# Two transformer blocks on one core: weight parts ahead of waits, tiles taken out of PSUM by ScalarE, and sums of squares on TensorE

## What is computed

```
h = x                                     # 1024 tokens, 1024 channels, fp32
h = h + hybrid_mixer(rmsnorm(h)) ; h = h + cross_attention(rmsnorm(h), mem)
h = h + (gelu(causal_dwconv(u[..., :F])) * u[..., F:]) @ w_down ; u = rmsnorm(h) @ w_up
x2 = rmsnorm(h, final_g)                  # F = 2816 here and below
z = rms_norm(x2) @ w_in_2                 # sliding window attention and an HGRN2 recurrence
h = x2 + rms_norm(concat([ya, yh]) @ w_out_2, g_mix_post_2)
h = h + rms_norm(cross_attention_2(rms_norm(h), m), g_x_post_2)
u = rms_norm(h, g_ffn_pre_2)
h = h + rms_norm((silu(u @ w_gate_2) * (u @ w_up_2)) @ w_down_2, g_ffn_post_2)
```

## Time and profile before

| | us |
|---|---|
| median of 3 runs | 2897.3 |
| lowest and highest | 2895.75, 2897.48 |
| the profiled execution | 2897.78 |
| its span | 2895.9 |
| TensorE busy | 2764.6 |
| DVE busy | 1813.2 |
| GpSimd busy | 1378.6 |
| ScalarE busy | 1012.2 |
| mean granted TensorE clock | 0.977 of full |

### The profile page before, as it was taken

The page is one execution under the profiler, slowest core; times in us unless marked ns, Lnnn a source line. Parts: engine busy times, 40 slices in busy tenths (PEclk is TensorE's granted clock), DMA queues, the critical chain, the costliest instruction groups (busy, mean ns, idle before and its releaser), DMA issues.

```text
span 2895.9 us, 36440 instructions
## 1 busy us (share of the span) xinstructions
PE 2764.6 (95%) x13206; PEld 2282.4 (79%) x13206; DVE 1813.2 (63%) x1944; ACT 1012.2 (35%) x1605; POOL 1378.6 (48%) x789
## 2 busy tenths in 40 slices
PE   7999899999999999999999998899997999999996
PEld 6888687887788888888887776678976888888884
DVE  7888542335876676766745547694479555655556
ACT  3257531332322222223323435353446222222223
POOL 4322212214666676665565330434153666566665
PEclk9999999999999999999999998899998999999998
DMA  4101222111111111113322110422023111111113
GB/s 147 37 23 52 80 96 79 36 59 51 44 51 47 54 47 62 51 46 114 110 89 87 37 44 1 153 87 89 15 95 110 55 51 58 54 43 58 47 61 124
DMA packets 71982, 191.25 MB, mean 66 GB/s; under 512 B 7760, under 2 KB 8016, under 8 KB 70864
## 3 DMA queue, kind: packets, MB, share of 16 engines
q1 hardware_dynamic: 59616, 152.92, 15.9%
q10 hardware_dynamic: 12272, 37.06, 3.4%
HBM read 172.65 MB, written 17.30 MB: 66 GB/s over the span
## 4 chain that ended last, share of the span: by engine, by line
PE 48%; issue 34%; POOL 14%; DVE 2%; ACT 1%; DMA 1%; POOLq 0%; SPq 0%; DVEq 0%; ACTq 0%
PE products L649 15%; PE products L1078 8%; PE others L1078 8%; PE products L1120 5%; PE others L1120 5%; POOL w_lo L550 4%; POOL w_lo L494 2%; POOL w_hi L491 2%; POOL w_raw L568 1%; POOL w_raw L566 1%; DMA w_raw<-wstream 1%; DVE work L2233 1%; POOL w_raw L557 1%; POOL part_sum L562 1%; PE products L769 1%
## 5 line engine op out<-in xcount | busy, mean ns | idle before, releaser
L550 POOL TENSOR_TENSOR w_lo<-w_raw,w_hi 128x512 fp32r<-128x512 f32 x328 | 457.3, 1399 | 457.0 <-ACT w_hi L1780 455.9
L1780 ACT ACTIVATE w_hi<-w_raw 128x512 fp32r<-128x512 f32 x328 | 207.7, 634 | 816.5 <-PE others L1078 207.6
L491 POOL TENSOR_TENSOR w_hi<-w_raw,small 128x1024 fp32r<-128x1024 f32 x56 | 113.9, 2034 | 641.6 <-PE products L649 357.2
L649 PE MATMUL products<-act_hi,w_hi 128*128 128x512 f32 x912 | 366.7, 402 | 5.7 <-issue 4.4
L649 PE MATMUL products<-act_lo,w_hi 128*128 128x512 f32 x912 | 357.3, 392 | 0.0
L649 PE MATMUL products<-act_hi,w_lo 128*128 128x512 f32 x912 | 357.2, 392 | 0.0
L494 POOL TENSOR_TENSOR w_lo<-w_raw,w_hi 128x1024 fp32r<-128x1024 f32 x96 | 253.5, 2641 | 165.3 <-ACT w_hi L2065 160.9
L649 PEld LDWEIGHTS products<-act_hi,w_hi 128*128 128x128 f32 x912 | 172.4, 189 | 48.8 <-issue 12.5
L649 PEld LDWEIGHTS products<-act_hi,w_lo 128*128 128x128 f32 x912 | 172.4, 189 | 37.2
L649 PEld LDWEIGHTS products<-act_lo,w_hi 128*128 128x128 f32 x912 | 172.8, 189 | 33.3 <-issue 0.2
L743 PE MATMUL products<-act_hi,w_hi 128*128 128x512 f32 x408 | 170.6, 418 | 18.5 <-DVE act_lo L3114 8.1
(11 more groups left out here) (534 smaller groups left out, 6907.7 us busy)
## 6 DMA issues: line engine op xcount, KB each, us to landing
w_raw<-wstream SPq DMA_DIRECT2D x155, 512.0 KB, 3.5
w_raw<-wstream SPq DMA_DIRECT2D x248, 256.0 KB, 2.6
work<-xT ACTq DMA_DIRECT2D x16, 512.0 KB, 8.1
parked<-work ACTq DMA_DIRECT2D x8, 512.0 KB, 3.0
work<-parked ACTq DMA_DIRECT2D x8, 512.0 KB, 8.8
parked<-work ACTq DMA_DIRECT2D x2, 2048.0 KB, 7.9
work<-parked SPq DMA_DIRECT2D x8, 512.0 KB, 7.7
out<-work ACTq DMA_DIRECT2D x16, 256.0 KB, 2.2
```

The costliest lines, as they stand in the source:

```text
L491: pool.tensor_tensor(w_hi[:, slot, :], w_raw[:, slot, :], zeros, ALU.add)\
L550: pool.tensor_tensor(ring_lo[slot], source, ring_hi[slot].bitcast(F32), ALU.subtract).then_inc(s(signal), 1)
L649: last = pe.matmul(out[:, c], a[:, ws, w], x[:, k, c], start=(k == 0 and i == 0), stop=(k == KT - 1 and i == 2))
L1780: act.activation(ring_hi[slot], source, ACT.Copy).then_inc(s("parts_high"), 1)
```

## The change

It touches six places.

1. Start: ScalarE makes the high parts of weight blocks 0 and 1, GpSimd only the low parts, and TensorE waits for block 1 only before its first product with it.
2. q1: value tile 0 leaves PSUM after the weight low of n = 13 instead of after all of them.
3. Both feed-forwards: at the entrance ScalarE makes the second high before the gates and the third to sixth ahead of copies and hidden parts. DVE makes the low parts of the fourth differences before the first hidden tiles. TensorE peels chunk 1 from its loop and waits there for fewer evacuated tiles.
4. out2 and xo2: ScalarE instead of DVE takes half tiles out of PSUM; in out2 the first three before its waits for the recurrence. Of the parked tiles, 4 to 7 and the scale are loaded in recurrence step 7, the scale into `W[:, 16]` instead of `rstd`; tiles 0 to 3 one by one behind the low parts. DVE computes residuals 4 to 7 first.
5. ffn2a, second half: TensorE itself sums the eight squares (`square_of`), one matmul for each, between the steps of the half tile; DVE's eight adds go. TensorE's first tile waits for one evacuation less.
6. ffn2 entrance: DVE evacuates the first tiles between sums and low parts in another order, and TensorE waits for low parts by thirds.

```diff
-            split(0, 0, 0)
-            split(1, 0, 1)
+            for b in range(2):
+                pool.wait_ge(s("weights_high"), b + 1)
+                pool.tensor_tensor(w_lo[:, b, :], w_raw[:, b, :], w_hi[:, b, :].bitcast(F32), ALU.subtract).then_inc(s("weights_split"), 1)
...
                 def first_pair():
-                    pe.wait_ge(s("weights_split"), b + 2)
                     for k in range(KT):
...
                         for j in range(2):
+                            if k == 0:
+                                pe.wait_ge(s("weights_split"), b + j + 1)
...
+                def square_of(k):
+                    pe.wait_ge(s("squares"), BEFORE_HALVES + HALF_SQUARED["ffn2", 1, k])
+                    c = half_of(1)
+                    pe.matmul(N[:, 0, c], ones, sq[k % 2][:, c], start=(k == 0), stop=(k == KT - 1)).then_inc(s("squares_summed"), 1)
...
                         half_tile(b + j, ff_slots[j][:, half_of(half)], half, half_operand("ffn2", half) if j == 0 else None,
-                                  (s("evacuated"), PROD0["xo2"] + 16) if j == 0 else None, beside)
+                                  (s("evacuated"), PROD0["xo2"] + 15 + half) if j == 0 else None, beside,
+                                  (lambda k: square_of(k - 1) if k else None) if (half, j) == (1, 0) else None)
+                        if (half, j) == (1, 0):
+                            square_of(KT - 1)
...
                     else:
-                        pe.wait_ge(s("evacuated"), of.evacuated(c, -2))
+                        pe.wait_ge(s("evacuated"), of.evacuated(c, -3 if first else -2))
...
-                    pe.wait_ge(s("diff_lo"), diffs + 12)
+                        pe.wait_ge(s("evacuated"), of.evacuated(c, -2 if first else -1))
+                    pe.wait_ge(s("diff_lo"), diffs + (4 if name == "ffn2" else 12))
...
+            def first_weights(b):
+                act.wait_ge(s(f"weights_loaded{b}"), 16)
+                act.activation(w_hi[:, b, :], w_raw[:, b, :], ACT.Copy).then_inc(s("weights_high"), 1)
+            first_weights(0)
             for k in range(KT):
+                if k == 1:
+                    first_weights(1)
...
-                    copied(c, 0)
-                    high(c, 4)
-                    high(c, 5)
-                    high(c, 6)
+                    if isinstance(c, int) and c == 1:
+                        high(c, 6)
+                        copied(c, 0)
...
                 high(1, 1)
+                high(1, 2)
                 gate(0, 0)
-                if name == "ffn1":
-                    gate(0, 1)
-                high(1, 2)
-                if name == "ffn2":
-                    gate(0, 1)
+                gate(0, 1)
+                high(1, 3)
...
-                high(1, 3)
+                high(1, 4)
+                high(1, 5)
                 hidden_high(1, 0)
...
+                if c == 7:
+                    act.wait_ge(s("hg_qk"), 3 * NCH)
+                    for k in range(4, KT):
+                        load(W[:, k, :], ap["parked"][:, k, :], f"x_in{k}")
+                    act.wait_ge(s("sw_o_lo"), 1)
+                    load(W[:, 16, :], parked_scale, "scale_moved")
...
+            def half_out(stage, u):
+                act.wait_ge(s("product_quarters"), 4 * (BLOCK0[stage] + u + 1))
+                act.activation(W[:, 8 + u % 8, half_of(u // 8)], half_slot(stage, u), ACT.Copy).then_inc(s("evacuated"), 1)
+            for u in range(3):
+                half_out("out2", u)
...
-            act.wait_ge(s("y2_lo"), 4 * len(hg_batches))
-            load(rstd[:, :], parked_scale, "scale_moved")
-            for k in range(KT):
+            for k in range(4):
+                act.wait_ge(s("y2_lo"), 4 + k + 1)
                 load(W[:, k, :], ap["parked"][:, k, :], f"x_in{k}")
...
                 for u in range(8):
                     high(u + 10)
+                    half_out(stage, 8 + u)
                     act.wait_ge(s("evacuated"), p + 8 + u + 1)
...
+                    sums_of(1)
+                    sums_of(2)
+                    dve.wait_ge(*half_total_of("roots", "ffn2", 1))
+                    first_tile(0)
+                    sums_of(3)
+                    first_tile(1)
+                    for k in range(4):
+                        third_lows(k)
+                    first_tile(2)
+                    for k in range(4):
+                        low_of_difference(1, k)
+                    first_tile(3)
+                    for k in range(4):
+                        low_of_difference(0, k)
+                last_lows()
+                first_hidden()
                 low_part(1, 0)
-                last_lows()
...
+                if n == KT + 5:
+                    value("1", 0)
...
-            for g in range(2):
-                value("1", g)
+            value("1", 1)
...
-                    half_sum(nxt, half, k)
+                    if (nxt, half) != ("ffn2", 1):
+                        half_sum(nxt, half, k)
                 for u in range(8):
-                    out_of(u)
-                    if u:
-                        half_sum(post, 0, u - 1)
+                    half_sum(post, 0, u)
                     beside(u)
-                half_sum(post, 0, 7)
                 for u in range(8):
-                    out_of(8 + u)
                     added(0, u)
...
             def residuals(u):
-                if u >= 4:
-                    residual(2 * u - 8)
-                    residual(2 * u - 7)
+                if u < 4:
+                    residual(4 + u)
+                elif u >= 6:
+                    residual(2 * u - 12)
+                    residual(2 * u - 11)
```

More of the change, by code:

```diff
@@ L730, in half_total, with half_tile @@
                 pe.matmul(N[:, 0, c], ones, ssum[:, c], start=True, stop=True).then_inc(s("token_sums"), 1)
-            def half_tile(b, out, half, ready=None, free=None, beside=None):
+            def half_tile(b, out, half, ready=None, free=None, beside=None, each=None):
                 pe.wait_ge(s("weights_split"), b + 1)
@@ L745, in half_tile @@
                         beside()
+                    if each:
+                        each(k)
                 last.then_inc(s("product_quarters"), 4)
@@ L1083, in pair @@
                     n, out = 7 * j, lambda m: bank(pair_banks[j][m])
+                    first = isinstance(c, int) and c == 1
                     if j:
@@ L1127, in ffn, with chunk @@
                     up(b, p, b, norm_sums(name), name, None, True)
-                with pe.Fori(1, FC) as c:
+                def chunk(c):
                     pair(c, 0)
@@ L1136, in ffn @@
                                   lambda k: g_hi[:, k, :], lambda k: g_lo[:, k, :])
+                chunk(1)
+                with pe.Fori(2, FC) as c:
+                    chunk(c)
                 def last_half(half):
@@ L1764, in high @@
                     free = (-4, -2, 0, 1, 2, 3, 4, 5, 6, 8, 9, 10, 11, 12, 13, 14, 16, 18)[n - 1]
+                    if isinstance(c, int) and (c, n) == (1, 2):
+                        free = -4
                     pair_, i = (n - 1) // 7, (n - 1) % 7
@@ L2125, in in_halves @@
                     high(u)
-            in_halves("out2", "pm", "q2", "x2", 31, h_made("residual", KT))
+            in_halves("out2", "pm", "q2", "x2", 31, 3)
             cross("2")
```

92 lines of the change are left out of this document (43 added, 49 removed).

## The result

| | before | after |
|---|---|---|
| median, us | 2896.53 | 2866.44 |
| lowest and highest of 4 runs | 2895.48, 2897.48 | 2866.28, 2866.8 |
| ratio, 95% interval | | 0.9896, 0.9879 to 0.9914 |
| the profiled execution, and its span | 2897.78, 2895.9 | 2866.35, 2864.3 |

A forecast was written before the change was run, and what follows sets the result against it. The prediction took TensorE to bound the kernel, busy 2764.6 of 2895.9 us, so only its idle time or slow pace could be won. Terms 3.3 + 6.0 + 3.4 + 18.6 + 12.0 = 43.3 us gave 2854, range 2845 to 2873.

The forecast's parts named there:

- A: First products: ScalarE's highs let TensorE start near 11 with block 0, block 1 at 14.0; gain 3.3 us (2.0 to 3.6).
- B: First query tile: moving value tile 0's copy removes TensorE's wait and slow pace; gain 6.0 us (3.8 to 6.6).
- C: First feed-forward: earlier ScalarE highs let GpSimd's chain of lows and product 5 come earlier; gain 3.4 us (1.5 to 4.5).
- The third low follows at 752.3: First feed-forward: GpSimd's third low comes behind ScalarE's third high, 3.4 us earlier than its 755.69 in before.
- D: Second mixer's output: ScalarE's evacuations and earlier residuals remove most idle time and slow pace; gain 18.6 us (12 to 22).
- E: Second feed-forward: evacuation wait goes, squares on TensorE, new orders; product 5 near 2242.5 instead of 2254.88; gain 12 (7 to 15).
- the circle: Second feed-forward's squared tile: ScalarE's third square waits for TensorE's first; tile ends some 4 us earlier, not 8.
- R1: DVE or ScalarE still sets the loops, evacuations only change hands; D gives 9, E 5; 2871 us; chance 0.17.
- R2: Waits between steps keep TensorE at half clock in the squared tile; E falls to 5; 2861 us; chance 0.15.
- R3: ScalarE evacuates behind waiting squares and highs, so half tiles come slower than 5.44 us; 2910 us; chance 0.04.
- R4: Orders change but the same late item, a DMA or semaphore, stays behind; within 0.2%, 2897 us; chance 0.04.

The follow-up runs named there:

- c6: The changed kernel with GpSimd making high and low parts of weight blocks 0 and 1 as before: 2868.7 us, 29.0 less than before.
- c1: The changed kernel with value tile 0 taken out of PSUM after all weight lows again: 2877.2 us, 20.5 less than before.
- a1: The changed kernel with ScalarE's sixth and seventh highs of chunk 1 ahead of the first hidden tile's high, both feed-forwards: 2867.6 us, 30.5 less than before.
- a5: The changed kernel with chunk 1's sixth to eighth highs (second feed-forward: also ninth) ahead of the copy of product 1: 2862.6 us, 36.4 less than before.
- c5: The changed kernel with DVE evacuating half tiles in out2 and xo2 again, parked tiles and residuals still early: 2887.2 us, 11.8 less than before.
- c4: The changed kernel with parked tiles, scale and residuals late as before, ScalarE still evacuating: 2871.2 us, 26.6 less than before.
- c3: The changed kernel with squares of the second feed-forward's second half summed by DVE again, one total on TensorE: 2865.2 us, 33.8 less than before.
- a2: The changed kernel with two of TensorE's eight sums of squares a half tile earlier, the others one step earlier: 2865.7 us, 32.4 less than before.
- a3: The changed kernel with the second feed-forward's first two chunk 1 highs ahead of the last two differences: 2867.3 us, 30.9 less than before.

## Why the prediction was right, and where not

**A, near in size, wrong in cause.** 2.5 us against 3.3, by the seventh matmul (14.80 against 17.34). The first matmul came at 12.07, not 11: ScalarE's table load began at 6.1, but its first copy of weights (7.38) then stood ahead of the first operand, and DVE's low operand took 2.51 us from 9.51. c6 shows that the highs on ScalarE were not needed.

**B, right.** 7.3 against 6.0 with an upper bound of 6.6. The wait went and the slow pace with it. The moved copy by itself is worth 5.2 in c1's trace, inside the bounds. The other 2.1 are a wait 0.7 longer in before than in c1, four more slow matmuls behind it (0.8), and two short waits for GpSimd's queue in v1 (0.32 and 0.53 us, of which c1 has one of 0.29). The slow pace is no fixed price: ten matmuls behind 4.41 us of waiting in before, six behind 3.68 in c1.

**C, the step that failed.** The gain at product 5 came, 3.08 us against 3.4, though not as the sum had it. "The third low follows at 752.3" was wrong: it came at 743.62, which with the 10.42 us gained before is 754.04, so 1.65 us earlier. The other 1.5 came because GpSimd took 6.33 us from the third to the fifth low where it had taken 7.85, which no term had: that was luck. The failed step is to book the gain at product 5 as a gain of the kernel. I didn't ask what is late next: the sixth high, which the change leaves behind the hidden tile, while it moves DVE's four last lows (6.42 us) ahead of that tile. Item 3 of "The change" has this wrong too: the sixth high stands ahead of the copy, but behind `hidden_high(1, 0)`; only the third to fifth stand ahead of it. The high part of that tile comes 8.6 us later than in before, measured from the roots of ffn1 (752.86 against 754.68 in the traces). a1 and a5 show the queue step by step, a5 how far it had to be cleared and what limits then. The net was +0.9, outside my bounds of 1.5 to 4.5, since these bounded the place and not the end.

**D, right, with luck.** 18.6 forecast; the stretch gave 19.3, of which 0.7 fall in the recurrence. At the place where the term ends, the second total (1925.62, now 1899.27), 16.1 were gained beside this 0.7; the other 2.5 are slow pace behind that total, which the term did not count. The split between its pieces was partly luck too: before the totals I had left 1 and 2.5 us, it was 2.78 and 0.99; I had seen no wait for GpSimd's lows (2.1). DVE's groups up to the first total, in the changed kernel (1820 to 1860 us) and then in before (1839 to 1880 us; its residual products are the earlier trace rows):

```profile
L3145 DVE TENSOR_TENSOR tmp<-tmp 128x512 f32<-128x512 f32 x7 | 13.4, 1911 | 0.2
...
L2848 DVE SCALAR_TENSOR_TENSOR work<-work,cols 128x1024 f32<-128x1024 f32 x8 | 13.3, 1684 | 0.0
```

```profile
L3085 DVE TENSOR_TENSOR tmp<-tmp 128x512 f32<-128x512 f32 x7 | 7.6, 1079 | 0.0
```

The residual products beside GpSimd fell from a mean of 2.28 to 1.68 us, but the seven sums rose from 1.08 to 1.91, where I had reckoned with 0.8. Together they took 25.6 us before and 26.7 after. So DVE was not made faster by moving the residuals; what left its queue are the evacuations. The Trainium skill, "SBUF — State Buffer", section "SBUF: two separate sides", has VectorE and GpSimd shut each other out there; these means, and the 1.30 and up to 2.28 us of the same GpSimd operation in a5, agree with that. c5 gives the evacuations 12.5 us of D, c4 about 1 to the loads. By subtraction some 5 are left. Perhaps they fall due only with both undone, but no run has both, and that is not shown.

**E, too large.** At product 5 8.6 against 12 (bounds 7 to 15). Two waits stand where I had less or none: 3.08 before the squared tile's third step, from the circle that I named and priced only in part, and 3.38 before product 1, whose high part I had not looked for behind the last differences. Then 5.8 were given back behind product 5, by the mechanism of C; a5 wins 3.1 of them back. DVE's new order and TensorE's waits by thirds (item 6) have no run of their own, so their share of the 8.6 is not shown.

**The rivals.** R1, that evacuations only change hands in the loops, put the gain in D at 9 us and E at 5; c5 gives the evacuations alone 12.5 in D and 7.1 in E. The measured time lies between R2's 2861 and R1's 2871, but came about by neither's way. The granted clock in the squared tile is 1.00, where R2 wanted half. Waits of 3.08 and then 0.83 us left TensorE at 2.4 GHz in this tile, while in c3 waits of 1.60 to 2.17 us went with 1.2 GHz. The Trainium skill ("TensorE: Matmul & The Clock Gate", in "HAM oscillation") tells of a kernel whose stretches of work start slow behind waits of 3 to 5 us. Neither tile here shows that: the changed one stayed fast behind 3.08 us, and c3's turned slow behind waits shorter than those. The measurement decides. R3 did not happen: ScalarE's evacuation takes 0.58 us and half tiles keep 5.44. R4 is excluded.

## What to carry to other kernels

A gain is worth what is left of it where the next queue lets go: follow it until an instruction that nothing in the change touched starts earlier, and price that one. In an in-order queue between two engines, moving two entries out of a wait can just move the wait by two (a1); look for the entry that waits for the slow engine and clear everything that others need from behind it. An edit that starts the slowest chain earlier (a2) keeps its gain, one that starts a chain with slack earlier (a3) doesn't.

## What the runs showed of the hardware

The same GpSimd operation on 128x512 took 1.30 us in some places and 1.74 or 2.28 in others. The four last lows on DVE took 6.42 us beside GpSimd's operations, where four of the same size took 2.50 (from 727.41 in the changed kernel), most of it while GpSimd stood still. Where both worked from SBUF, both were slower, and eleven GpSimd operations took 20.6 us in a5 instead of 14.3. No order tried here removed that: the chain took 20.3 us in before, too. No run isolates it, so this is read from rows that lie beside each other. And TensorE's clock stayed at 2.4 GHz in a tile that waited at three of its steps for 0.83 us and once for 3.08, while the same tile with waits of 1.60 to 2.17 us (c3) went down to 1.2 GHz.
